# A new preamble for a two-layer trunk: x's norm in columns, modulation in two pairs, three slabs k by k

## The reference

```python
c_act = jax.nn.silu(c)
mod = c_act @ ada_w[l] + ada_b[l]
sh1, sc1, g1, sh2, sc2, g2 = jnp.split(mod, 6, axis=-1)
h = rms_norm(x, norm_mix_g[l]) * (1 + sc1) + sh1
proj = h @ w_in          # b_gate, c_gate, u, q, k, v, g
y = b_gate * causal_conv3(c_gate * u)    # the first part of the mixer
```

## Time and profile before

| | us |
|---|---|
| median of 3 runs | 2659.22 |
| lowest, highest | 2650.5, 2659.87 |
| profiled execution, its own time | 2665.52 |
| its span | 2663.7 |
| mean granted clock of TensorE | 0.975 |
| TensorE busy | 2539.8 |
| VectorE busy | 1343.7 |
| ScalarE busy | 562.7 |
| GpSimd busy | 975.3 |

### The profile page before, as it was taken

How to read it: one execution, slowest core, us unless ns; L and a number is a source line. 1 busy time by engine, 2 the same in 40 slices (tenths; PEclk the granted TensorE clock), 3 DMA queues, 4 the chain that set the end, 5 groups by cost and what they waited for, 6 DMA issues and landing times.

```text
span 2663.7 us, 34189 instructions
## 1 busy us (share of the span) xinstructions
PE 2539.8 (95%) x11374; PEld 2081.5 (78%) x11374; DVE 1343.7 (50%) x2095; ACT 562.7 (21%) x1023; POOL 975.3 (37%) x1604
## 2 busy tenths in 40 slices
PE   2999999999999999999889999997999999999999
PEld 2688778888788788788678888875878888888887
DVE  5735777464434433443757777786552222222233
ACT  3201322220000000000456666662210000000001
POOL 1553333444434344346132222241444444444440
PEclk7899999999999999999989999997999999999999
DMA  7243446422222222222211111114111111111111
GB/s 282 84 150 101 133 131 222 132 71 78 73 79 79 69 80 80 63 79 71 79 36 37 36 32 44 32 49 157 32 48 52 51 47 47 51 51 47 47 32 63
DMA packets 220583, 208.31 MB, mean 78 GB/s; under 512 B 6059, under 2 KB 165957, under 8 KB 220357
## 3 DMA queue, kind: packets, MB, share of 16 engines
q1 hardware_dynamic: 202708, 164.13, 20.0%
q10 hardware_dynamic: 17776, 43.00, 4.4%
HBM read 183.00 MB, written 24.12 MB: 78 GB/s over the span
## 4 chain that ended last, share of the span: by engine, by line
PE 88%; DVE 7%; issue 2%; ACT 2%; DMA 1%; SPq 0%; ACTq 0%; DVEq 0%
PE psG L606 26%; PE psG L612 26%; PE psG L611 26%; PE psM L925 1%; PE psG L966 1%; DVE n_t L1526 1%; PE psZ L955 1%; PE psO L606 1%; PE psO L611 1%; PE psO L612 1%; DVE h_lo L1518 1%; DVE hid_hi L1451 1%; DVE ada_acc L1575 1%; PE psZ L606 1%; PE psZ L612 1%
## 5 line engine op out<-in xcount | busy, mean ns | idle before, releaser
L606 PE MATMUL psG<-h_hi,w_split 128*128 128x512 f32 x2496 | 992.4, 398 | 27.0 <-DVE h_lo L1453 13.8
L611 PE MATMUL psG<-h_lo,w_split 128*128 128x512 f32 x2496 | 978.1, 392 | 0.0
L612 PE MATMUL psG<-h_hi,w_split 128*128 128x512 f32 x2496 | 977.6, 392 | 0.0
L585 POOL TENSOR_SCALAR w_split<-w_raw 128x256 fp32r<-128x256 f32 x800 | 364.9, 484 | 1613.9 <-PE psG L606 517.3
L589 POOL TENSOR_TENSOR w_split<-w_raw,w_split 128x256 fp32r<-128x256 f32 x800 | 619.5, 807 | 0.0
L606 PEld LDWEIGHTS psG<-h_hi,w_split 128*128 128x128 f32 x2496 | 471.7, 189 | 137.6 <-issue 17.9
L612 PEld LDWEIGHTS psG<-h_hi,w_split 128*128 128x128 f32 x2496 | 471.9, 189 | 100.9
L611 PEld LDWEIGHTS psG<-h_lo,w_split 128*128 128x128 f32 x2496 | 472.4, 189 | 98.3 <-issue 4.1
L1812 DVE TENSOR_TENSOR hid<-sil,psG 128x512 f32<-128x512 f32 x88 | 60.5, 688 | 724.4 <-PE psG L612 721.8
L1828 DVE SCALAR_TENSOR_TENSOR xT<-psG,mod,xT 128x512 f32<-128x512 f32 x352 | 259.7, 748 | 173.9 <-PE psG L612 173.7
L1056 ACT ACTIVATE sil<-psG 128x512 f32<-128x512 f32 x88 | 52.5, 599 | 1311.5 <-PE psG L612 1311.5
(11 more groups left out here) (189 smaller groups left out, 2052.9 us busy)
## 6 DMA issues: line engine op xcount, KB each, us to landing
ada_raw<-in_ada_w SPq DMA_DIRECT2D x80, 512.0 KB, 4.0
w_raw<-in_ffn_w_gate SPq DMA_DIRECT2D x44, 512.0 KB, 3.7
w_raw<-in_ffn_w_up SPq DMA_DIRECT2D x44, 512.0 KB, 3.7
w_raw<-in_ffn_w_down SPq DMA_DIRECT2D x44, 512.0 KB, 3.7
w_raw<-in_ev_w_in SPq DMA_DIRECT2D x28, 512.0 KB, 4.2
w_raw<-in_od_w_qkv SPq DMA_DIRECT2D x24, 512.0 KB, 3.7
ada_first<-in_ada_w SPq DMA_DIRECT2D x4, 2048.0 KB, 12.6
x_spill<-xT ACTq DMA_DIRECT2D x2, 4096.0 KB, 15.3
```

What stands on the lines that cost most here:

```text
L585: nc.gpsimd.tensor_scalar(slot[:, 0, part], raw[:, part], 1.0, 1.0, ALU.mult, ALU.mult).then_inc(hi_done, 1)
L606: mm = nc.tensor.matmul(o, st[0], mv[0], start=first, stop=False, **kw)
L611: nc.tensor.matmul(o, st[0], mv[1], start=False, stop=False, **kw)
L612: return nc.tensor.matmul(o, st[1], mv[0], start=False, stop=end, **kw)
```

## The change

**Loads.** The nine constants go out from ScalarE's queue, ahead of its table load. SP begins with half 0 of x, then groups 0 and 2 in two pieces each (now four buffers, eight semaphores), slabs 0 and 1, half 1 of x, slab 2, groups 1 and 3, ada pieces 0 and 1. The buffers of groups 0 and 3 lie in the slots of slabs 2, 3 and 4, 5, so GpSimd waits for the sums before it splits those. The rest of SP's order stays.

**Norm.** ScalarE squares x as it was loaded (tokens on partitions) and sums along the row with accum_out: one column for 128 tokens, four instructions for a half. Root and Newton work on 128 x 4. Then ScalarE scales the identity by each column, and TensorE multiplies a matrix of ones with it: the root stands spread over the partitions in PSUM (psO, psZ), where `h_tile` reads it. The adds, `norm_pe`, `norm_root` and the large Newton are gone for this norm.

**Modulation.** Order 0, 2, 1, 3. After each pair TensorE makes 8 columns, VectorE shift, scale and gain of four tiles (`first_mod`). Tiles 0 to 3 of half 0 are made after the first pair, tiles 4 to 7 after the second.

**First six steps.** TensorE multiplies slabs 0 and 1 with tiles 0 to 3, k by k, turns half 1 of x through two other banks, multiplies slab 2 with tiles 0 to 3, makes the second pair's columns and half 1's root, then all three slabs k by k with tiles 4 to 7, then all three with half 1. ScalarE's copy and VectorE's z of the first step (`conv_copy`, `conv_z`) are moved between the second and third tile of half 1.

```diff
@@ sync
+            load_x(0)
+            first_ada(0)
+            first_ada(2)
...
+                        if phase == "conv" and first(i) and s < 2:
+                            if s == 1:
+                                load_x(1)
+                            continue
+                        if phase == "conv" and first(i) and s == 2:
+                            first_ada(1)
+                            first_ada(3)
+                            ada("conv", 0, 0)
+                            ada("conv", 0, 1)
@@ gpsimd
+                        if phase == "conv" and s == 2:
+                            pool.wait_ge(ada_first_sum, KT)
+                        if phase == "conv" and s == 4:
+                            pool.wait_ge(ada_first_sum, KT * FIRST_ADA)
@@ tensor
+            def x_root_pe(h):
+                pe.wait_ge(x_dg, 4 * h + 4)
+                for j in range(4):
+                    mm = nc.tensor.matmul(x_root[h][:, P * j:P * j + P], consts[:, 5], x_diag[h][:, j], start=True, stop=True)
+                mm.then_inc(x_root_in, 1)
+            def first_cols(n):
+                pe.wait_ge(ada_first_sum, 2 * KT * (n + 1))
+                misc("norm0", 0, n, [lambda k=k, q=q: nc.tensor.matmul(
+                    psM[:, 4 * n + 8 * q + k:4 * n + 8 * q + k + 1], first_acc[q][:, k], consts[:, 5, 0:1], start=True, stop=True)
+                    for q in range(2) for k in range(4)])
...
+            x_root_pe(0)
+            first_cols(0)
+            def first_conv():
+                def k_major(h, slabs, ks):
+                    for k in ks:
+                        for s in slabs:
+                            proj("conv", 0, 3 * h + s, s, h, hT, only=(k,), ready=h_wait("norm0", h) if s == slabs[0] else None)
+                            if h == 1 and k == KT - 1:
+                                used("conv", 0, 3 + s)
+                k_major(0, (0, 1), range(4))
+                pe.wait_ge(x_nat_in[1], 16)
+                for k in range(KT):
+                    if k >= 2:
+                        pe.wait_ge(x_copied, k - 1)
+                    for j in range(4):
+                        mm = nc.tensor.transpose(x_bank[k % 2][:, P * j:P * j + P], x_nat[:, 4 + j, P * k:P * k + P], ident)
+                    mm.then_inc(x_turned, 1)
+                k_major(0, (2,), range(4))
+                first_cols(1)
+                x_root_pe(1)
+                k_major(0, (0, 1, 2), range(4, KT))
+                k_major(1, (0, 1, 2), range(KT))
@@ scalar
+            def x_squares(h):
+                act.wait_ge(x_nat_in[h], 16)
+                for n in range(4 * h, 4 * h + 4):
+                    if n:
+                        act.wait_ge(x_sq, n)
+                    fn(x_junk[:], x_nat[:, n], ACT.Square, accum_out=x_col[0][:, n:n + 1]).then_inc(x_sq, 1)
...
+            x_squares(0)
+            x_column_root(0)
+            for k in range(KT):
+                act.wait_ge(gemm_done, k + 1)
+                fn(xT[:, k, half(0)], psG[:, k % BANKS], ACT.Copy).then_inc(bank_read[k % BANKS], 1)
+            x_diagonal(0)
+            for k in range(4):
+                norm_hi("norm0", 0, k)
+            for k in range(KT):
+                act.wait_ge(x_turned, k + 1)
+                fn(xT[:, k, half(1)], x_bank[k % 2], ACT.Copy).then_inc(x_copied, 1)
+            x_squares(1)
+            x_column_root(1)
+            x_diagonal(1)
...
+            for k in range(4, KT):
+                norm_hi("norm0", 0, k)
+            spill("norm0", lambda: act.wait_ge(x_copied, KT))
...
             for k in range(KT):
                 norm_hi("norm0", 1, k)
+                if k == 1:
+                    conv_copy(0, 0, 0)
@@ vector
-            for g in range(FIRST_ADA):
-                first_sum(g)
-                if g == 0:
-                    norm0.newton(0)
-
-                ada_cols("norm0", 0, 1 + g, 4 * g)
-                if g == 1:
-                    for k in range(KT - 1):
-                        norm0.add(1, k)
-            dve.wait_ge(misc_read, M("norm0", 0, FIRST_ADA))
-            mod_gain(0, 0, 1)
-            dve.wait_ge(gemm_done, 16)
...
+            first_sum(0, 0)
+            x_newton(0)
+            first_sum(0, 1)
+            first_sum(1, 0)
+            first_sum(1, 1)
+            first_mod(0)
...
+            dve.wait_ge(x_root_in, 1)
+            for k in range(4):
+                norm0.h_tile(0, k)
+            norm0.low(0, 3)
+            for n in (2, 3):
+                for q in range(2):
+                    first_sum(n, q)
+            x_newton(1)
+            first_mod(1)
+            for k in range(4, KT):
+                norm0.h_tile(0, k, k > 4)
+            dve.wait_ge(x_copied, KT)
+            dve.wait_ge(x_root_in, 2)
+            for k in range(KT):
+                norm0.h_tile(1, k)
+                if k == 1:
+                    conv_z(0, 0, 0)
```

More of the change, by code:

```diff
@@ L94 @@
 PHASES = [
-    ("start", 1, dict(step=16, misc=2)),
-    ("norm0", 1, dict(misc=6)),
+    ("start", 1, dict(step=8, misc=2)),
+    ("norm0", 1, dict(misc=2)),
     ("conv", 2, dict(slab=6, step=12, misc=1, ada=4)),
@@ L264, in build @@
         const_in = sem("const_in")
-        x_nat_in = sem("x_nat_in")
+        x_nat_in = [sem(f"x_nat_in{n}") for n in range(NH)]
+        x_sq = sem("x_sq")
+        x_rs = sem("x_rs")
+        x_newt = sem("x_newt")
+        x_dg = sem("x_dg")
+        x_root_in = sem("x_root_in")
+        x_turned = sem("x_turned")
+        x_copied = sem("x_copied")
         c_split = sem("c_split")
@@ L277, in build @@
         misc_read = sem("misc_read")
[L278 removed]
+        ada_first_in = [sem(f"ada_first_in{n}") for n in range(2 * FIRST_ADA)]
         ada_first_sum = sem("ada_first_sum")
@@ L618, in misc, with proj @@
                 got.then_inc(misc_done, 1)
-            def proj(phase, i, s, slab, h, src, sub=0, kts=KT, part=None, ready=None):
+            def proj(phase, i, s, slab, h, src, sub=0, kts=KT, part=None, ready=None, only=None):
                 b = bank(phase, s)
@@ L1518, in low, with h_tile @@
                     V.scalar_tensor_tensor(lo, n_t[k % 2][:], sh, hi.bitcast(F32), ALU.add, ALU.subtract).then_inc(h_ready, 1)
-                def h_tile(self, h, k):
+                def h_tile(self, h, k, low=True):
                     l, which = divmod(self.q, 2)
+                    root = n_r[:] if self.q else x_root[h]
                     e = KT * (2 * self.q + h) + k
-                    if k >= 2:
+                    if k >= 2 or self.q == 0 and h:
                         dve.wait_ge(h_ready, e - 1)
-                    V.scalar_tensor_tensor(n_t[k % 2][:], xT[:, k, half(h)], modA[:, 2 * l + which, k:k + 1], n_r[:], ALU.mult, ALU.mult).then_inc(n_ht, 1)
-                    if k:
+                    V.scalar_tensor_tensor(n_t[k % 2][:], xT[:, k, half(h)], modA[:, 2 * l + which, k:k + 1], root, ALU.mult, ALU.mult).then_inc(n_ht, 1)
+                    if k and low:
                         self.low(h, k - 1)
@@ new lines, in first_mod @@
+            def first_mod(n):
+                c = 4 * n
+                dve.wait_ge(misc_done, M("norm0", 0, n))
+                V.tensor_tensor(mod[:, KT + c:KT + c + 4], psM[:, 8 + c:12 + c], vecA[:, KT + c:KT + c + 4], ALU.add).then_inc(first_scale, 1)
+                V.tensor_tensor(mod[:, c:c + 4], psM[:, c:c + 4], vecA[:, c:c + 4], ALU.add).then_inc(misc_read, 1)
+                dve.wait_ge(first_scale, n + 1)
+                V.scalar_tensor_tensor(modA[:, 0, c:c + 4], mod[:, KT + c:KT + c + 4], 1.0, vecA[:, V_NORM + c:V_NORM + c + 4],
+                                       ALU.add, ALU.mult).then_inc(gain_ready, 1)
+                dve.wait_ge(gain_ready, n + 1)
+                dve.wait_ge(misc_read, M("norm0", 0, n))
@@ new lines, in conv_z @@
+            def conv_z(i, j, h):
+                s = 6 * j + 3 * h + 1
+                dve.wait_ge(gemm_done, G("conv", i, s))
+                bank_wait(dve, "conv", i, s - 1)
+                if h == 0:
+                    dve.wait_ge(tap, ONE + 6 * j + 3 * h + 12 * i)
+                z = zb[:, 2 + H * h:2 + H * h + H]
+                V.tensor_tensor(z, csb[h][:], psG[:, bank("conv", s)], ALU.mult).then_inc(bank_read[bank("conv", s)], 1)
+            first_sum(0, 0)
+            x_newton(0)
```

150 lines of the change are left out of this document (83 added, 67 removed).

## The result

The changed kernel takes 2626.52 us (median of 6 runs, 2620.21 to 2636.8), the kernel before 2651.76 in the same rounds (6 runs, 2646.45 to 2659.87): a ratio of 0.9897, 95% interval 0.9879 to 0.9916. The medians differ by 25.2 us; 26 was forecast, and 2633 us with a range of 2620 to 2648. The profiled execution is the fastest of the six: 2620.21, its span 2618.4 against 2663.7.

What follows compares the result with a forecast made beforehand. TensorE, busy 95% of the span, bounds the kernel, so only its idle or slow-clocked stretches count. Six steps 31.0 us earlier less 5.0 for slab 4 give 26.0: median 2659.22 to 2633 us, range 2620 to 2648.

Steps and rivals of the forecast that it cites:

- sixth step ends: End of conv's first six steps (j = 0, both halves): 83.6 us against 114.6, 31.0 earlier; bounds 78 to 92.
- slab 4's wait, with its clock: One step behind the sixth: slab 4 comes late, a 4.2 us wait plus 0.8 for the clock, together 5.0 given back.
- the squares hidden inside the sums: Before the first gain: ScalarE's four squares, 4.4 us, fit inside VectorE's 11.9 us of sums.
- ScalarE sets the second pair: Second pair of modulation groups: ScalarE behind the transposes ends last, at 53.4 us; VectorE's sums end at 50.
- If those squares are cheaper by a fifth it gives 1 us: ScalarE's squares of x's second half: a fifth cheaper gives 1 us, with 3 us available before VectorE's sums take over.
- The 0.8 for the clock: Allowance for TensorE's clock falling in the gap before slab 4: 0.8 us, bounds 0 and 3.
- The two groups of h_hi of half 0: Sign of being right: h_hi of half 0 appears in two groups of four, about 20 us apart.
- (a): Rival at the start: constants late behind SP's loads, c_act ready at 23 us; gain about 15, 2644 us; chance 0.09.
- (b): Rival in the first steps: TensorE's clock stays low in pieces between waits; gain about 15, 2644 us; chance 0.10.
- (c): Rival: clock at 0.50 for all of j = 0 and the step behind slab 4's gap; about 2667 us; chance 0.02.
- (d): Rival, more gain: slab 4 lands in 3.9 us, columns at high clock, n_t not stretched; 2626 us; chance 0.09.
- All further slabs are paced by TensorE as before: nothing: Slabs behind slabs 4 and 5: nothing gained or lost there.

Runs made afterwards that it cites:

- experiment 5: Changed kernel with all four modulation groups summed and turned to columns before the first tile; median 2633.18 us, ratio 0.9916 to the kernel before.
- experiment 3: Changed kernel with ScalarE's squares and root of x's half 1 moved ahead of half 1's copies; median 2625.33 us, ratio 0.9884 to the kernel before.
- experiment 4: Changed kernel with the first steps' products slab by slab instead of k by k; median 2620.45 us, ratio 0.9864 to the kernel before.
- Experiment 2: Changed kernel with slabs 4 and 5 issued earlier, ahead of the third and fourth ada pieces; median 2621.02 us, ratio 0.9884 to the kernel before.
- experiment 6: Changed kernel with fifteen dead 128x512 VectorE adds put back among the sums; median 2641.75 us, ratio 0.9957 to the kernel before.
- experiment 9: Changed kernel with half 0's root copied from PSUM to SBUF by ScalarE and read there by the tiles; single run 2622.83 us.
- experiment 1: Changed kernel run again without any edit; median 2629.62 us, ratio 0.9902 to the kernel before.

## Why the prediction was right

The time, the sign and the mechanism hold: 25.2 us between the medians, 28.0 at the mark. By its own steps, forecast against the profile after:

| step | forecast | measured |
|---|---|---|
| c_act; group 0's half in | 10; 12.0 | 12.2; 12.58 |
| sums of the first pair end; first gain done | 25.0; 29.6 | 26.65; 30.8 |
| first burst of 24 ends | 41.0 | 41.9 |
| half 1 copied; squares and root done | 48.5; 53.4 | 47.7; 52.7 |
| sums of the second pair end; second gain done | 50; 55.2 | 51.36; 55.4 |
| first product on tile 4; sixth step ends | 57.5; 83.6 | 58.24; 83.7 |
| slab 4's wait, with its clock | 4.2 + 0.8 | 2.8 + 0 (here) |

**The path.** The sixth step ended within 0.1 us of the forecast, but partly by errors that cancel. *Late:* VectorE idles 1.21 us at 16.64 for ScalarE, whose squares wait for the constants' activations and pay 0.19 us extra each for reading the accumulator; the forecast had the squares hidden inside the sums. *Early:* transposes went at 0.67 us a tile, not 0.86; the burst ahead of them had raised the clock (without the burst, in experiment 5, the first ones go at 0.85 to 0.95). Half 1's copies and squares so ended 0.7 ahead of the forecast, and its Newton step used that up: the first three 128x4 instructions took 0.65 instead of 0.2 beside GpSimd's subtraction. *As forecast:* the columns at the low clock (3.59 for 3.8), the first pair of tiles, and the burst with its clock up at about 39.4.

**ScalarE sets the second pair.** True in the profile, but the margin over VectorE's sums was 1.4 us (52.73 against 51.36) and not 3, and with it taken away experiment 3 gained 0.3 us on tile 4's start against experiment 4, which ran at the same clock. The term that the prediction lacked is a third chain: the columns, which wait for the sums, and which take 1.95 or 3.57 by TensorE's clock. In experiments 2, 3 and 4 they took 3.35 to 3.57 and ended no earlier than 0.4 us before the Newton step. The sentence "If those squares are cheaper by a fifth it gives 1 us" is the part of the prediction that wasn't borne out.

**Slab 4.** The wait appeared where forecast, behind one step, for w_split. 1.4 of its 4.2 us weren't there: ada's first piece ended at 80.2, 3.5 before the sixth step's end as worked out, but the load took 6.2 us from issue (80.77 to 86.94), not 7.2, and the split 4.85 instead of 4.92; the rest is hand-over. The 0.8 for the clock was a fair mean: of the eight profiles with this wait the clock fell behind it in four, at 1.3 to 1.6 us each. Experiment 2 confirms the wait: without it the mark is 2.6 earlier.

**What was too small.** The prediction has no term for the adds; it lies in the difference of two chains. Measured alone it is 13.4 us, 12.1 of them ahead of slab 4, where the expectation of experiment 6 said 8 to 9, since later sums also fall beside GpSimd and the columns run at the low clock.

**A sign that came out otherwise.** The two groups of h_hi of half 0 start at 31.62 and 56.37, 25 us apart and not about 20; the prediction's own times for the two first tiles (32.0 and 57.5) are 25 apart as well, so this sign had been put down wrongly.

**The rivals.** (a) refuted: c_act was late by 2 us, at a cost under 1. (b) and (c): the clock was back at 39.4 and 60.0. It came back 1 to 2 us later than at 60.0 in experiments 2, 3 and 4, and a fall behind slab 4's wait cost 1.3 to 1.6; both also happen in runs whose edit touches neither place. The mechanism is real, its size was small. (d) came true in part: n_t wasn't stretched. By the Trainium skill (SBUF — State Buffer, Who interferes with whom) one SBUF input, outside VectorE's two-port modes, doesn't contend with GpSimd; for n_t the trace agrees, 0.75 against 1.09 us in experiment 9. As the prediction gives the rule, without the part on the modes, it doesn't hold for every instruction: the cast of experiment 1 has one SBUF input and was blocked for 10.05 us.

**"All further slabs are paced by TensorE as before: nothing".** This fits the medians, but not the two profiled executions: the prediction counted from the profile of before, whose stretch behind the mark was 17.4 us longer, 11.1 of it waits for blocked VectorE. So its span of 2637.7 for the profile after came out as 2618.4.

**Open.** What sets off the long blocks, and what decides when in the first burst the clock comes back (37.3 to 39.6 us). GpSimd's splits spaced out, or the hidden tiles kept in PSUM, were not tried.

## What to carry to other kernels

Cost a change at the start by one mark behind it (here the end of the sixth step and the next slab), and read that mark, not the span, in every experiment: whole executions of one kernel differed by 17 to 31 us, the two marks of the same kernel by 0.2, and a fall of the clock on the way adds 1.3 to 1.6. An engine that ends last gives no more when relieved than the distance to the next chain, and here that distance hung on TensorE's clock: price both chains at both clocks. Before a low clock is put down to an edit, look whether it stands in runs without that edit too. When a stage is pulled forward, look for the load that was just in time before; it becomes the next wait, and one reordered issue mends it.

## What was unexpected in the hardware

- One VectorE instruction can be blocked for very long beside GpSimd: 5.98 and 10.05 us for a 128x512 cast from SBUF (0.43 in the median) and 14.27 for a subtraction (0.69). The last one spans GpSimd's splits of three whole slabs and the end of a fourth, some 25 instructions in a row. It differs from execution to execution, and the profiled stretches behind the mark follow it.
- 128x4 instructions of VectorE took 0.63 to 0.65 us beside GpSimd's subtraction and 0.17 without it (52.76, and 16.64).
- Behind TensorE's wait of 2.6 to 2.7 us for slab 4 its clock had fallen in four of eight profiles; what follows then ran at 0.43 us a matmul for about 3 us.
- The granted clock in the windows isn't to be read before the first change that the trace records: it stands at 1.00 up to 52 us after, while products at 34 to 39 us started 0.43 apart, the pace of the low clock.
- ScalarE's activation with a sum along the row is two instructions, 1.06 us for 128x1024 and 0.19 to read the sum.
